# The indexer's transposes between the halves of the sparse attention's product, the lambda row behind the next product

## The reference, cut to what matters

```
h = x @ w_in                                   # q, k, v of two attentions, and the indexer's iq, ik, iw
lam = exp(sum(lp[0]*lp[1])) - exp(sum(lp[2]*lp[3])) + lam_init
ya = diff_attention(dq, dkk, dv, lam)          # uses lam after its softmax
iq, ik = partial_rope(iq), partial_rope(ik)
dots  = einsum('bqhd,bsd->bqhs', iq, ik) * 64 ** -0.5
score = einsum('bqhs,bqh->bqs', relu(dots), iw)     # masked to s <= q
_, sel = top_k(score, 64)
yb = sparse attention of sq, sk, sv over sel
```

## Time and profile before

| | |
|---|---|
| median of three executions | 1995.1 us |
| the profiled execution's own time | 1992.25 us |
| its span, first to last instruction | 1990.4 us |
| mean granted clock of TensorE | 0.989 |
| PE busy | 1901.8 us (96%) |
| DVE busy | 1410.8 us (71%) |
| ACT busy | 1078.4 us (54%) |

### The profile page before, as it was taken

How to read it: one execution, slowest core, us unless ns; L and a number is a source line. 1 busy time by engine, 2 the same in 40 slices (tenths; PEclk the granted TensorE clock), 3 DMA queues, 4 the chain that set the end, 5 groups by cost and what they waited for, 6 DMA issues and landing times.

```text
span 1990.4 us, 31257 instructions
## 1 busy us (share of the span) xinstructions
PE 1901.8 (96%) x12624; PEld 1731.5 (87%) x12624; DVE 1410.8 (71%) x2301; ACT 1078.4 (54%) x1694; POOL 67.1 (3%) x78
## 2 busy tenths in 40 slices
PE   7989989999999999899998899999999999999998
PEld 6879869999888898699997789998999889998997
DVE  6876878888778867798887666675445666675444
ACT  5454557777555545677774554444444555444442
POOL 1000000000000000000000000000000000000001
PEclk9999989999999999999999999999999999999999
DMA  7426169999544262799994433345555533445552
GB/s 294 148 86 233 50 252 415 386 406 420 219 170 148 107 233 72 301 411 376 421 421 160 157 137 136 128 162 184 188 190 180 186 137 107 136 182 171 189 190 85
DMA packets 61047, 426.73 MB, mean 214 GB/s; under 512 B 6960, under 2 KB 7088, under 8 KB 11872
## 3 DMA queue, kind: packets, MB, share of 16 engines
q1 hardware_dynamic: 59760, 421.65, 55.9%
q0 software_dynamic: 416, 1.81, 0.3%
q10 hardware_dynamic: 720, 1.19, 0.2%
HBM read 423.58 MB, written 1.05 MB: 213 GB/s over the span
## 4 chain that ended last, share of the span: by engine, by line
PE 81%; DVE 13%; ACT 3%; DMA 1%; issue 1%; POOL 0%; DVEq 0%; ACTq 0%; SPq 0%
PE bank L1097 67%; PE scp L1097 11%; DVE WSl L1459 4%; PE bank L1330 1%; ACT SC L2102 1%; ACT WSh L2049 1%; PE bank L1207 1%; DVE sm L1607 1%; DMA ring<-wts 1%; PE bank L1234 1%; PE bank L1176 1%; DVE scp L1605 1%; POOL sm L2294 0%; DVE XTl L1712 0%; DVE sm L1412 0%
## 5 line engine op out<-in xcount | busy, mean ns | idle before, releaser
L1459 DVE TENSOR_TENSOR WSl<-ring,WSh 128x1024 fp32r<-128x1024 f32 (+3 forms) x512 | 590.0, 1197 | 193.6 <-ACT WSh L2049 192.7
L2049 ACT CAST WSh<-ring 128x1024 fp32r<-128x1024 f32 (+3 forms) x512 | 498.0, 1026 | 184.7 <-PE bank L1097 92.7
L1097 PE MATMUL bank<-XTh,WSh 128*128 128x256 f32 x1216 | 349.4, 287 | 3.6 <-DVE GT L1727 2.5
L1097 PE MATMUL bank<-XTl,WSh 128*128 128x256 f32 x1216 | 345.7, 284 | 0.0
L1097 PE MATMUL bank<-XTh,WSl 128*128 128x256 f32 x1216 | 345.5, 284 | 0.0
L1097 PE MATMUL bank<-WSh,FA 128*128 128x512 f32 (+1 forms) x848 | 303.6, 391 | 2.3 <-DVE FA L1927 1.2
L1097 PE MATMUL bank<-WSl,FA 128*128 128x512 f32 (+1 forms) x680 | 263.4, 387 | 0.0
L1097 PEld LDWEIGHTS bank<-XTh,WSh 128*128 128x128 f32 x1216 | 234.8, 193 | 6.2 <-DVE WSl L1459 3.0
L1097 PEld LDWEIGHTS bank<-XTl,WSh 128*128 128x128 f32 x1216 | 234.9, 193 | 0.2
L1097 PEld LDWEIGHTS bank<-XTh,WSl 128*128 128x128 f32 x1216 | 234.7, 193 | 0.0
L1097 PE MATMUL bank<-WSh,XTh 128*128 128x512 f32 (+4 forms) x544 | 202.8, 373 | 18.8 <-DVE WSl L1459 17.0
(11 more groups left out here) (293 smaller groups left out, 2905.4 us busy)
## 6 DMA issues: line engine op xcount, KB each, us to landing
ring<-wts SPq DMA_DIRECT2D x264, 1024.0 KB, 4.9
V<-wts SPq DMA_DIRECT2D x40, 1024.0 KB, 12.9
PT<-wts SPq DMA_DIRECT2D x30, 1024.0 KB, 8.9
H<-wts SPq DMA_DIRECT2D x28, 1024.0 KB, 9.4
GT<-wts SPq DMA_DIRECT2D x12, 1024.0 KB, 13.2
A<-wts SPq DMA_DIRECT2D x8, 1024.0 KB, 7.5
ring<-wts SPq DMA_DIRECT2D x8, 584.0 KB, 7.2
ring<-wts SPq DMA_DIRECT2D x4, 832.0 KB, 8.3
```

The costliest lines, as they stand in the source:

```text
L1097: return nc.tensor.matmul(dst, lhsT, rhs, start=start, stop=stop)
L1459: nc.vector.tensor_tensor(lo[:, c], buf[:, c], hi[:, c].bitcast(F32), ALU.subtract).then_inc(*lo_done.inc(("block", i)))
L2049: nc.scalar.copy(hi[:, c], buffers[s.buffer][:, c]).then_inc(*hi_done.inc(("half", i, k)))
```

## The change

Two steps move. The indexer's transposes now stand between the two products of sq, with everything they issue: 10 transposes on PE and three copies on ACT and DVE. `lambda` now stands behind the product dq, that is between the scores of t = 0 and those of t = 1, again with everything it issues: two matmuls on PE, the table load (layer 0 only) and the exponent on ACT, five operations on DVE. Nothing is added or removed in arithmetic. Behind the moved steps the banks are numbered differently; the turns of ACT and DVE stay as they were.

```
@@ -343,11 +343,13 @@
         self.add("rope", name="iq", l=l)
-        self.columns("w_in", "sq", l, W1["sq"], 1024, src)
+        for c in range(2):
+            for f in self.wide("w_in", "sq", l, c, W1["sq"] + 512 * c, 512, src):
+                f()
+            if c == 0:
+                self.turn("IT", l, 10, P)
         if l == 0:
             self.add("rows")
-        self.add("lambda", l=l, u=self.bank("dve"))
-        self.turn("IT", l, 10, P)
         self.add("rope", name="sq", l=l)
...
             if t == 0:
                 self.pace = 12
                 self.columns("w_in", "dq", l, W1["dq"], 512, src)
+                self.add("lambda", l=l, u=self.bank("dve"))
```

## The result

The changed kernel takes 1996.76 us (median of 20 executions, 1994.68 to 1998.30), the kernel before 1992.32 us in 20 executions beside them (1991.05 to 1996.86). The ratio is 1.0017, with a 95% interval of 1.0011 to 1.0024, that is 3.4 us (2.2 to 4.8). The medians lie further apart, 4.4 us: of the twenty executions of the kernel before, thirteen lie at 1991.05 to 1992.98 and seven at 1995.08 to 1996.86 with none between, so its median sits in the lower group. The means are 3.5 us apart. The profiled execution took 1995.64 us, with a span of 1993.8 us and a mean granted clock of 0.987.

A forecast was written before the change was run, and what follows sets the result against it. From the relu of t = 1 on, DVE's queue was taken to bound the kernel, not PE. Layer 0 -0.9 + 1.2, layer 1 +1.5 + 0.5: +2.3 on 1992.25, plus 2.85 for the median, about 1997 us; range 1991 to 2001.

The forecast's parts named there:

- PE's early gain: PE ahead of the scores of t = 0: stops, lambda row and low clock go, 3.81 us in layer 0, 1.90 in layer 1.
- The cover of the transposes: Second product of sq: 1.31 us of moved transposes hide ACT's 0.6 us bank copy; without it 0.6 us lost per layer.
- the third rival: Second product of sq waits for ACT's bank copy or a slipped split: 0.6 us per layer, +1.2, 1998 us; chance 0.07.
- PE as the bound: PE sets the time, its 6.1 us come through whole: 1989 us, 0.3% faster; chance 0.07 together with a weaker form.
- The relu behind the exponent: ACT's relu of t = 1 waits for lambda behind 24 DVE index steps: 0.9 us earlier in layer 0, 1.5 later in layer 1.
- DVE's idle time of 1.7 us: DVE before the split behind the relu of t = 1, layer 0: idle time stays near 1.7 us.
- The weaker form of the first rival: Lambda does not hold back the relu, only DVE's earlier start counts: -5.3 us, 1990; chance 0.07 together with PE-bound form.
- The clock behind the new stops: Low clock after PE's longer stops: +1.2 us at layer 0's gate product, +0.5 at layer 1's scores of the other attention.
- The second rival: Layer 0's whole gate product at 1.2 GHz, layer 1's 2 us beyond its cover: +9.1 us, 2004; chance 0.06.
- the base of layer 0: Layer 0's low clock, taken as removed by the change: 0.76 us at scores of t = 0, 0.82 in dq.

## Why the prediction was right, and the step of it that was off

**The time** was forecast at 1997.0, within no change of 0.3%; it is 1996.76. Part of this is luck: I forecast +2.3 us on the profiled execution and added 2.85 us for the median of three. Over 20 executions the kernel before has 1992.32, level with its profiled 1992.25, so that this offset didn't exist, and the difference is +3.4 by the ratio. Put on 1992.32, the forecast's +2.3 would have given 1994.6, 2.1 us under what was measured.

**PE's early gain** came as worked out: from ACT's first copy to the scores of t = 0 it is 30.88 us now against 34.17, 3.3 us less in layer 0 (3.05 from the stops and the row), and 28.83 against 30.77 in layer 1, 1.9 (1.90). The cover of the transposes held, so the third rival (0.6 us a layer) fell: with the transposes alone PE has no new stop there and layer 1 gains 1.75 us to the diff scores. **PE as the bound** fell too: its gain is in the trace, and the two later stops have grown by 6.6 us (4.33 + 3.94 - 0.81 - 0.88).

**The relu behind the exponent** is the mechanism, and it was predicted with its direction in layer 1: +1.5 forecast, +1.3 measured (46.28 against 45.00 us from ACT's first copy there). The idle time of DVE is 2.35 us where I said 2.3. In layer 0 the relu was forecast at 66.6 and came at 66.75, of which about 0.6 is the later first copy of ACT (17.99 against 17.43); against the profile that I had it is 1.2 us earlier (0.9 forecast), and up to the diff scores layer 0 is level with that profile (83.04 and 83.04 on average, +0.3 forecast). DVE's idle time of 1.7 us there came out at 2.35. I carried over the 1.65 of the earlier trace rows where it should have been worked out: the split begins 2.82 to 2.85 us behind the relu in both layers of both kernels, and in the changed kernel DVE is ready about 0.5 us behind it, so the idle time must be the same in both layers. The 1.65 wasn't the usual value either; in the other profiles of the kernel before it is 0.80 to 0.85, as in layer 1. The sum didn't use this term. The weaker form of the first rival, in which lambda does not hold back the relu, fell with ACT's 3.56 and 4.43 us ahead of the exponent; it needs lambda out of that place.

**The clock behind the new stops** was forecast at +1.2 and +0.5 us and measured at +1.3 (7.28 - 5.99) and +0.5 (1.24 - 0.73). Filling the stops took both away and 1.7 us with them. The second rival, the whole gate product at 1.2 GHz, didn't come; the worst seen is 8.43 us, in the kernel with the new place in layer 0 alone. The 1.7 us are about half of the loss. The rule of the Trainium skill, "TensorE: Matmul & The Clock Gate", section "HAM oscillation — how this bites in real kernels", that a long enough gap makes the next burst start at the low clock, agrees with the granted clock of 0.73 and 0.50 behind the two stops.

**The step that failed** is the base of layer 0. "and the clock, 1.92 - 1.16 = 0.76" and "0.82 more from the clock in dq", 1.58 us together, stand in the sum as something that the change takes away. They were an accident of one profile: three of four executions of the kernel before run at 1.00 there. Against the usual execution the relu of layer 0 is 0.3 us later (48.75 against 48.43) and not 0.9 earlier, and layer 0 costs 1.6 us and not 0.3. With that the sum is +1.6 in layer 0 and +1.8 in layer 1, +3.3 us with rounding, where the ratio says 3.4.

**What stays open.** The time from layer 0's diff scores to layer 1 is about 1.1 us shorter in the changed kernel (459.4 against 460.2 to 460.7), although both its profiles have a low stretch at 120 to 128 us (granted clock 0.79) that three of the four of the kernel before don't have; and behind layer 1 it differs by up to 2.5 us between executions of one kernel. Low stretches move there, at 659 or 688 us for one. Why they move wasn't tried, and their parts cancel only roughly.

## What to carry to other kernels

When a step is moved down an in-order queue, ask on every engine what it will stand behind and what behind it: 1.4 us of DVE's work, put behind 24 index steps, held back ACT's relu and casts by over 3 us, for a result that is needed much later. Before such a step is moved because it makes another engine wait, see whether what it waits for (here PR) can be made earlier. A stretch at the low clock in one profile may be missing in the next, so take a second one, or carry both cases, before a sum takes it away.

## What the runs showed of the hardware

Whether the clock falls behind a stop, and for how long, is only roughly told by the stop. Behind one stop of 0.80 to 1.18 us before the gate product the clock stayed at 1.00 in all of eight profiles (four of the kernel before, the transposes alone, and the three with an early PR). Behind one stop of 2.44 us (lambda behind the relu) it fell, and the gate product took 7.47 us:

```profile
89.45 7.47 PE bank L1100 x48
```

Behind 3.86 us it took 8.19, behind 4.32 to 4.33 us once 8.43 and twice 7.24 to 7.28. In layer 1 the sixteen scores behind the stop took 1.68 us behind 2.06 us, 1.36 behind 3.91 and twice 2.08 behind 3.94, where they take 1.16 at 1.00. So the same stop was followed by more or less low clock in different kernels, and by the same in two executions of one. And two stops of 1.53 and 1.31 us, with 1.3 us of transposes between them, let it fall in one execution of four.

The table load for the exponent takes 1.28 us on ACT and lay in its idle time nearly wherever it was put: behind the relu too (64.98 above), where the exponent then waited 0.32 us for DVE alone. The exception is the kernel with the rows step early and lambda ahead of the scores. There the exponent follows the load at once, and DVE waits 0.90 us for it:

```profile
50.18 1.28 ACT L2091 ACT_TABLE_LOAD   x1
51.48 0.20 ACT L2091 ACTIVATE sm<-sm 128x2 f32<-128x2 f32 x1
...
51.71 0.16 DVE L1567 TENSOR_TENSOR sm<-sm 128x1 f32<-128x1 f32 x1 [0.90 <-ACT sm L2091]
```

Its layer 0 is 0.3 us longer than with lambda between the blocks (78.71 against 78.40), where the load stands well ahead of the exponent; that the load causes this isn't shown.
